# Expert weights in twelve 1 MB transfers instead of six of 2 MB, in a Mixture-of-Experts decoder layer

## The chip, the core and the metric

One core of one Trainium2 chip runs the whole program. The metric is the device time of one execution in microseconds (us), from launch to the last output. The kernel before takes 1163.84 us, the median of 3 runs (1163.27 to 1166.18).

## The reference

One layer of a hybrid decoder trunk for 256 prompt tokens and 8 x 8 sample tokens, 320 in all, of width 1024. First a mixer (a projection `u = x @ w_in`, a gated short convolution, a gated linear recurrence, `@ w_out`, a LayerNorm). Then a Mixture of Experts: each token goes to 4 of 32 experts, and this part takes most of the time. All data are float32.

```python
g = xblk @ wg[e] + bg[e]
up = xblk @ wu[e] + bu[e]
g = jnp.minimum(g, SWIGLU_LIMIT)
up = jnp.clip(up, -SWIGLU_LIMIT, SWIGLU_LIMIT)
glu = g * jax.nn.sigmoid(SWIGLU_ALPHA * g)
return ((up + 1.0) * glu) @ wd[e] + bd[e]
```

Each expert has three matrices (gate, up, down) of 1024 x 1024 float32, 4 MB each, so 12 MB an expert and 384 MB for the 32. Every expert is read once from device memory.

## The kernel before

The mixer runs from 0 to about 184 us. While it runs, the six slots of `ring` serve the projection weights first and then take the matrices of expert 0.

The experts run after it as a loop of *units*. A unit is one expert and up to 64 of its tokens. There are 33 units for 32 experts: one expert has more than 64 tokens and takes two units, one after the other, on the same weights. A unit on TensorE is: gate product, first half; the result sum of the unit before (`combine`); gate product, second half; up product, two halves; gathering of the next unit's tokens (L1146); some transposes; down product, two halves (L1193 is the matmul of all six halves).

`ring` holds one expert: 6 slots of 16 KB a partition, 2 MB each. Slots 0 and 1 are the two halves of the gate matrix, 2 and 3 of up, 4 and 5 of down. In a slot a partition holds 4 whole rows of the matrix, which lie one after the other in device memory, so that a slot is 128 runs of 16 KB. There is no second buffer: a slot is loaded with the next expert's half as soon as the last unit of the present expert has finished its matmuls on it.

The sync engine (SP) issues all weight loads from one queue, in slot order. For each slot it waits until TensorE has counted that slot as used (`half_used` for a first half, `gate_done`, `up_done`, `y_done` for a second), then issues the load (L268, L269). TensorE in turn waits at the head of each half for the load's arrival (L1187), in `product`. `PRIOR` only corrects the count for the loads that the same slots took during the mixer.

GpSimd loads two small bias rows per unit (L369) on its own queue. Everything else of a unit lies on VectorE, ScalarE and GpSimd beside TensorE.

Of the kernel before, what the change touches and what calls it, by code (L numbers as in the profile page):

```python
# [27 lines left out]
SLOTW = 4 * D  # L28
NSLOT = 6
# [17 lines left out]
LOGIT_BANKS = [1, 7, 3]  # L47
SUM_BANKS = [(5, 6), (7, 4), (2, 2)]
SUM_ORDER = (0, 1, 2)
PRIOR = [0, 0, 0, 3, 2, 2]  # L50


def hybrid_layer(nc, a):
# [3 lines left out]
    with ExitStack() as ctx:  # L57
# [3 lines left out]
        def sem(name):  # L61
            return ctx.enter_context(nc.semaphore(name))


        ring = sb("ring", [P, NSLOT, SLOTW])
# [94 lines left out]
        xTu = carve(P, HALF)  # L160
        hTu = carve(P, HALF)
# [30 lines left out]
            "ln2_centred ln2_var ln2_rstd ln2_norm out_dma dve_step act_step pool_step").split()}  # L192
        slot_loaded = [sem(f"slot_loaded{i}") for i in range(NSLOT)]
        x_in, x1_ok, ln2_ok = ([sem(f"{n}{t}") for t in range(3)] for n in ("x_in", "x1_ok", "ln2_ok"))
        half_used = [sem(f"half_used{m}") for m in range(3)]
        product_done = ["gate_done", "up_done", "y_done"]

        block = ctx.enter_context(nc.Block())
        w_in_v = a["w_in"][0].rearrange("(c p) n -> p c n", p=P)
# [4 lines left out]
        def slot_src(s, e):  # L204

            m = experts[s // 2]
            rows = m[e, (s % 2) * HALF:(s % 2 + 1) * HALF, :] if isinstance(e, int) else \
                m[bass.ds(e, 1), (s % 2) * HALF:(s % 2 + 1) * HALF, :].rearrange("o k n -> (o k) n")
            return rows.rearrange("(p c) n -> p (c n)", p=P)

        def slot(s):
            return ring[:, s, :].rearrange("p (c n) -> p c n", n=D)
# [8 lines left out]
        @block.sync  # L221
        def _(sp):

            for t, (t0, n) in enumerate(TILES):
                src = a["x_prompt"][0, t0:t0 + n, :] if t < 2 else a["x_sample"].rearrange("b s d -> (b s) d")
                sp.dma_start(x[0:n, t, :], src).then_inc(x_in[t], 16)

            for i, (g, s) in enumerate(IN_GROUPS[:3]):
                first_col = g * CW
                if i == 0:  # L230
                    first_col += 2 * P
                    sp.dma_start(ring[:, s, :].rearrange("p (c n) -> p c n", n=CW)[:, :, 0:2 * P],
                                 w_in_v[:, :, g * CW:first_col]).then_inc(S["first_cols"], 16)
                if i == 1:
                    sp.wait_ge(S["params_in"], 16 * 11)
                sp.dma_start(ring[:, s, :].rearrange("p (c n) -> p c n", n=CW)[:, :, first_col - g * CW:CW],
                             w_in_v[:, :, first_col:(g + 1) * CW]).then_inc(slot_loaded[s], 16)

            for s in range(3):
                sp.dma_start(ring[:, s, :], slot_src(s, 0)).then_inc(slot_loaded[s], 16)  # L240
            for i, (g, s) in enumerate(IN_GROUPS[3:]):
                sp.wait_ge(S["proj_done"], CT * (i + 1))
                sp.dma_start(ring[:, s, :].rearrange("p (c n) -> p c n", n=CW),
                             w_in_v[:, :, g * CW:(g + 1) * CW]).then_inc(slot_loaded[s], 16)
            sp.wait_ge(S["proj_done"], 3 * CT)
            sp.dma_start(slot(5), w_out_v[:, CT:CH, :]).then_inc(slot_loaded[5], 16)
            sp.wait_ge(S["proj_done"], 4 * CT)
            sp.dma_start(slot(3), w_out_v[:, 0:CT, :]).then_inc(slot_loaded[3], 16)
            for s, done, count in ((4, "proj_done", 5 * CT), (5, "lru_psum", 3), (3, "out_psum", 3)):
                sp.wait_ge(S[done], count)  # L250
                sp.dma_start(ring[:, s, :], slot_src(s, 0)).then_inc(slot_loaded[s], 16)
            for t in range(3):
                sp.wait_ge(x1_ok[t], 1)

            sp.wait_ge(S["out_psum"], 3)
            sp.dma_start(down_bias, a["exp_b_down"][0].rearrange("e (a n) -> e a n", a=4))\
                .then_inc(S["down_bias_in"], 16)
            for v, name in ((ln_g, "ln2_g"), (ln_b, "ln2_b")):
                sp.dma_start(v[:, :], a[name].partition_broadcast(P).rearrange("p o n -> p (o n)"))\
                    .then_inc(S["ln2_in"], 16)  # L260
            sp.wait_ge(S["tab_ok"], 1)

            def expert_load(e, before):

                used = sp.value_load(units_through[0:1, before], min_val=1, max_val=MAXU)
                for s in range(NSLOT):

                    sp.wait_ge(half_used[s // 2] if s % 2 == 0 else S[product_done[s // 2]], used)  # L268
                    sp.dma_start(ring[:, s, :], slot_src(s, e)).then_inc(slot_loaded[s], 16)  # L269

            expert_load(1, slice(0, 1))
            with sp.Fori(2, NE) as e:
                expert_load(e, bass.ds(e - 1, 1))
            for t in (1, 0, 2):
                t0, n = TILES[t]
                sp.wait_ge(ln2_ok[t], 1)
                dst = a["y_prompt"][0, t0:t0 + n, :] if t < 2 else a["y_sample"].rearrange("b s d -> (b s) d")
                sp.dma_start(dst, total[0:n, t, :]).then_inc(S["out_dma"], 16)
            sp.wait_ge(S["out_dma"], 48)
            sp.wait_ge(S["states_dma"], 96)  # L280
# [707 lines left out]
        def _(pe):  # L988
# [3 lines left out]
            for t, (t0, n) in enumerate(TILES):  # L992
                pe.wait_ge(x_in[t], 16)
                for c in range(CH):
                    b, col = (2 * t + c // 4, (c % 4) * P) if t < 2 else (4, c * n)
                    last = nc.tensor.transpose(bank[b][:, col:col + n], x[0:n, t, c * P:(c + 1) * P],
                                               ident[0:n, 0:n])
# [32 lines left out]
            for gi, (g, s) in enumerate(IN_GROUPS):  # L1030
                seen[s] += 1
                w = ring[:, s, :].rearrange("p (c n) -> p c n", n=CW)
                for j in range(CT):
# [7 lines left out]
                    for c in range(CH):  # L1041
                        last = mm(bank[j][:, 0:T], w[:, c, j * P:(j + 1) * P], xT[:, c, :],  # L1042
                                  start=c == 0, stop=c == CH - 1)
# [33 lines left out]
            for t in range(3):  # L1077
# [3 lines left out]
                if t == 0:  # L1081
# [3 lines left out]
                    for j in range(CT):  # L1085
                        last = nc.tensor.transpose(bank[6][0:OUTS, j * P:(j + 1) * P], states[:, j, 0:OUTS],
                                                   ident[:, :])
# [48 lines left out]
            for t, (t0, n) in enumerate(TILES):  # L1136
                last = mm(bank[6][:, 3 * NE:4 * NE], ones_bf[0:n, :], chosen[0:n, t, :],
                          start=t == 0, stop=t == 2)
# [38 lines left out]
            for t, (t0, n) in enumerate(TILES):  # L1177
                last = nc.tensor.transpose(bank[5][0:NE, t0:t0 + n], gate_of[0:n, t, :], ident[0:n, 0:n])
# [2 lines left out]
            pe.wait_ge(S["tab_ok"], 1)  # L1181
            n_last = pe.value_load(last_unit[0:1, 0:1], min_val=NE - 1, max_val=MAXU - 1)

            def product(b, m, left, s, e, between=None):

                for hf in range(2):
                    pe.wait_ge(slot_loaded[2 * m + hf], e * 16 + 16 * (PRIOR[2 * m + hf] + 1))  # L1187
                    w = slot(2 * m + hf)
                    for c in range(4):
                        lhsT = left[:, c * P + hf * UT:c * P + hf * UT + UT]  # L1190
                        end = hf == 1 and c == 3
                        for side in range(2):
                            last = mm(bank[b][side * UT:(side + 1) * UT, :], lhsT,  # L1193
                                      w[:, c, side * HALF:(side + 1) * HALF],
                                      start=m == 2 and hf == 0 and c == 0, stop=end, skip_group_check=True)
                    if hf == 0:
                        last.then_inc(half_used[m], 1)
                        if between:
                            between()
                last.then_inc(S[s], 1)  # L1200

            def biased(b, m):

# [30 lines left out]
            def unit(u, e, results):  # L1234

                pe.wait_ge(S["xu_ok"], u + 1)
                pe.wait_ge(S["gu_split"], u + 1)
                pe.wait_ge(S["gate_free"], u + 1)
                biased(0, 0)
                product(0, 0, xTu, "gate_done", e, between=results)  # L1240
                biased(1, 1).then_inc(S["gu_bias_used"], 1)
                product(1, 1, xTu, "up_done", e)
                pe.wait_ge(S["parts_ok"], 3)
                pe.wait_ge(S["low_zero"], 1)
                pe.wait_ge(S["member_ok"], u + 2)
                gather()
                pe.wait_ge(S["total_ok"], u * 3 + 3)
                pe.wait_ge(S["gated_ok"], u + 1)
                for t, (t0, n) in enumerate(TILES):
                    last = nc.tensor.transpose(bank[5][:, t0:t0 + n], gated[0:n, t, :], ident[0:n, 0:n])  # L1250
                last.then_inc(S["spread_psum"], 1)
                pe.wait_ge(S["hid_ok"], u + 1)
                transposed(4, hid, "hu_psum")
                pe.wait_ge(S["rows_ok"], u + 2)
                transposed(3, x_rows, "xu_psum")
                pe.wait_ge(S["hu_ok"], u + 1)
                product(2, 2, hTu, "y_done", e)

            pe.wait_ge(S["sel_ok"], 3)
            unit(0, 0, gated_biases)  # L1260
# [31 lines left out]
```

## Time and profile before

| what | us |
|---|---|
| median of 3 runs | 1163.84 |
| the profiled execution | 1164.26 |
| its span, first to last instruction | 1162.6 |
| TensorE matmuls, busy | 1086.0 (93%) |
| weight transfers, all loads of the sync queue | 86.5% of 16 engines' span |
| VectorE busy | 513.0 (44%) |
| GpSimd busy | 338.2 (29%) |
| ScalarE busy | 198.5 (17%) |

The page divides the span into 40 slices of 29 us and gives for each how busy every engine was and how many GB/s the 16 transfer engines moved. Its chain of waits follows the work back from the last instruction; there a "DMA" piece runs from the issue of a transfer to its landing. A matmul busy on the page is not a matmul at its peak: its end is modelled, and float32 matmuls appear as two records each, so a half product of 8 matmuls is 16 records.

### The profile page before, as it was taken

How to read it: one execution, taken by the hardware profiler on the slowest of the kernel's cores; microseconds unless marked ns; L12 is line 12 of the kernel's file. 1: busy time of each engine (PE TensorE's matmuls, PEld its weight loads, DVE VectorE, ACT ScalarE, POOL GpSimd, SP SyncE). 2: the span in 40 equal slices, each digit the busy share in tenths (PEclk: the TensorE clock that was granted, in tenths of full speed). 3: DMA queues.
4: the chain of work that ended last, by engine and by line, in shares of the span. 5: the costliest groups of instructions: out<-in, count | busy, mean ns of one | idle time of the engine just before them, and what ended most of it. 6: DMA issues, size and time to landing. Idle time of an engine off the chain costs nothing.

```text
span 1162.6 us, 14222 instructions
## 1 busy us (share of the span) xinstructions
PE 1086.0 (93%) x5219; PEld 436.7 (38%) x5220; DVE 513.0 (44%) x763; ACT 198.5 (17%) x322; POOL 338.2 (29%) x260
## 2 busy tenths in 40 slices
PE   7999947999999999999999999999999999999993
PEld 5766422333333333333333333333333333333330
DVE  4236386444444444444444444444444444444445
ACT  1151041111111111111111111011111111111111
POOL 2001131333333333333333333333333333333331
PEclk9999967999999999999999999999999999999997
DMA  9923233999999859999999999999999999999971
GB/s 319 358 73 145 77 114 102 429 426 429 428 428 427 366 219 427 428 430 426 429 427 429 427 429 427 429 428 428 428 428 429 427 429 427 429 428 429 427 334 45
DMA packets 41130, 423.29 MB, mean 364 GB/s; under 512 B 7839, under 2 KB 10015, under 8 KB 16542
## 3 DMA queue, kind: packets, MB, share of 16 engines
q1 hardware_dynamic: 36112, 421.15, 86.5%
q10 hardware_dynamic: 2766, 1.69, 0.5%
q0 software_dynamic: 2240, 0.30, 0.2%
q8 instruction: 7, 0.11, 0.0%
q14 instruction: 5, 0.04, 0.0%
HBM read 421.69 MB, written 1.42 MB: 364 GB/s over the span
## 4 chain that ended last, share of the span: by engine, by line
PE 61%; DMA 32%; DVE 4%; issue 1%; ACT 1%; SPq 0%
PE bank L1193 39%; DMA ring<-in_exp_w_up 31%; PE bank L1042 8%; PE bank L1229 5%; PE bank L1062 3%; PE bank L1146 3%; PE bank L1163 1%; ACT area L593 1%; PE bank L1250 1%; DMA ring<-in_w_in 1%; PE bank L1205 1%; PE bank L1155 0%; DVE area L960 0%; PE bank L1217 0%; PE bank L1023 0%
## 5 line engine op out<-in xcount | busy, mean ns | idle before, releaser
L1193 PE MATMUL bank<-ring,area 128*64 128x512 f32 x3168 | 713.9, 598 | 17.0 <-ACT area L593 8.9
L1193 PEld LDWEIGHTS bank<-ring,area 128*64 128x64 f32 x3168 | 225.0, 137 | 457.8 <-issue 427.6
L943 DVE TENSOR_TENSOR area<-bank,area 128x512 f32<-128x512 f32 (+1 forms) x204 | 128.4, 684 | 400.4 <-PE bank L1229 393.0
L382 POOL TENSOR_TENSOR bias_parts<-area,zero_col 2x1024 bf16<-2x1024 f32 x34 | 64.1, 1887 | 618.4 <-PE bank L1205 612.4
L886 DVE TENSOR_SCALAR member<-iota_s,unit_base,area 128x64 bf16<-128x64 f32 x99 | 130.1, 1367 | 0.0
L1229 PE MATMUL bank<-area 64*128 64x512 f32 (+1 forms) x396 | 98.8, 615 | 0.8 <-ACT area L599 0.8
L1042 PE MATMUL bank<-xT,ring 128*128 128x320 f32 x320 | 90.1, 442 | 2.6 <-DMA ring<-in_w_in 2.6
L393 POOL TENSOR_TENSOR bias_parts<-area,bias_parts 2x1024 bf16<-2x1024 f32 x34 | 78.8, 2317 | 4.9
L385 POOL TENSOR_TENSOR area<-area,bias_parts 2x1024 f32<-2x1024 f32 x34 | 72.6, 2136 | 5.2 <-POOL bias_parts L382 0.5
L589 ACT ACTIVATE area<-area 128x512 f32<-128x512 f32 x33 | 20.8, 631 | 311.4 <-DVE area L951 311.4
L1042 PEld LDWEIGHTS bank<-xT,ring 128*128 128x128 f32 x320 | 62.1, 195 | 28.9 <-issue 4.5
L390 POOL TENSOR_TENSOR bias_parts<-area,zero_col 2x1024 bf16<-2x1024 f32 x34 | 64.1, 1886 | 2.1
L591 ACT COPY area<-bank 128x512 f32<-128x512 f32 x33 | 19.4, 587 | 256.0 <-PE bank L1146 256.0
L1146 PE MATMUL bank<-area,member 128*64 128x512 bf16 x528 | 62.6, 379 | 0.0
L599 ACT COPY area<-bank 128x512 f32<-128x512 f32 x33 | 19.3, 586 | 214.2 <-PE bank L1193 214.2
L957 DVE TENSOR_SCALAR area<-bank 128x512 f32<-128x512 f32 x33 | 22.8, 691 | 74.2 <-PE bank L1193 74.2
L1229 PEld LDWEIGHTS bank<-area 64*128 64x128 f32 (+1 forms) x396 | 29.2, 167 | 68.1 <-issue 68.1
L1163 PE MATMUL bank<-ident,area 128*128 128x128 f32 x268 | 41.7, 298 | 10.3 <-DVE area L960 9.9
L892 DVE TENSOR_SCALAR area<-member,area 128x128 f32<-128x128 bf16 x99 | 42.6, 483 | 19.1 <-PE bank L1250 19.1
L951 DVE TENSOR_SCALAR area<-bank 128x512 f32<-128x512 f32 x33 | 22.8, 692 | 57.0 <-PE bank L1193 57.0
L960 DVE SCALAR_TENSOR_TENSOR area<-area 128x512 f32<-128x512 f32 x33 | 45.9, 1391 | 1.1
L1146 PEld LDWEIGHTS bank<-area,member 128*64 128x64 bf16 x528 | 30.8, 110 | 39.4 <-issue 19.7
(225 smaller groups left out, 549.8 us busy)
## 6 DMA issues: line engine op xcount, KB each, us to landing
ring<-in_exp_w_gate SPq DMA_DIRECT2D x64, 2048.0 KB, 21.2
ring<-in_exp_w_up SPq DMA_DIRECT2D x64, 2048.0 KB, 22.6
ring<-in_exp_w_down SPq DMA_DIRECT2D x64, 2048.0 KB, 20.7
ring<-in_w_in SPq DMA_DIRECT2D x4, 2048.0 KB, 15.8
ring<-in_w_out SPq DMA_DIRECT2D x2, 2048.0 KB, 7.8
ring<-in_w_in SPq DMA_DIRECT2D x2, 1024.0 KB, 11.2
x<-in_x_prompt SPq DMA_DIRECT2D x2, 512.0 KB, 4.0
out_y_prompt<-area SPq DMA_DIRECT2D x2, 512.0 KB, 3.1
```

The source lines that it names most:

```text
L382: g.tensor_tensor(bias_parts[0:2, :, :], whole, zero, ALU.add).then_inc(S["high_ok"], 1)
L385: g.tensor_tensor(rest, whole, bias_parts[0:2, :, :], ALU.subtract).then_inc(S["rest_ok"], 1)
L390: g.tensor_tensor(bias_parts[32:34, :, :], rest, zero_32, ALU.add).then_inc(S["mid_ok"], 1)
L393: g.tensor_tensor(bias_parts[64:66, :, :], rest, bias_parts[32:34, :, :], ALU.subtract)\
L886: last = v.tensor_scalar(dst[:, t, :], iota_s[:, :], unit_base[:, u], place[:, t, e], ALU.add, ALU.is_equal)
L943: last = v.tensor_tensor(total[0:n, t, cols], src, total[0:n, t, cols], ALU.add)
L960: v.scalar_tensor_tensor(hid, up_clip, 1.0, g_min, ALU.add, ALU.mult).then_inc(S["hid_ok"], 1)
L1042: last = mm(bank[j][:, 0:T], w[:, c, j * P:(j + 1) * P], xT[:, c, :], start=c == 0, stop=c == CH - 1)
L1146: last = mm(bank[3][side * UT:(side + 1) * UT, :], member[:, k // 3, :], x_parts[:, k, side * HALF:(side + 1) * HALF], start=k == 0, stop= ...
L1163: last = nc.tensor.transpose(bank[b][:, c * P:(c + 1) * P], src.rearrange("p (k c) -> p c k", c=4)[:, c, :], ident[:, :])
L1193: last = mm(bank[b][side * UT:(side + 1) * UT, :], lhsT, w[:, c, side * HALF:(side + 1) * HALF], start=m == 2 and hf == 0 and c == 0, stop ...
L1229: last = mm(b[0:n, :] if t < 2 else b[UT * h_:UT * h_ + UT, :], spread[UT * h_:UT * h_ + UT, t0:t0 + n], y_rows[UT * h_:UT * h_ + UT, :], ...
```

## The change

Each 2 MB slot is now loaded by two transfers of 1 MB, called quarters (a quarter of a matrix). Quarter 0 of a slot is the first 8 KB of each partition (rows 0 and 1 of its four), quarter 1 the last 8 KB. In device memory the 128 runs of a quarter are 8 KB long, 16 KB apart. Each quarter has its own semaphore of arrival (`quarter_loaded`) and its own semaphore of release (`quarter_used`; the last quarter of a matrix keeps the old name). TensorE waits before matmuls c = 0 and c = 2 of each half, and counts after c = 1 and c = 3. The matmuls, their order and the layout in `ring` are the same. With own semaphores for the arrival of experts' quarters, `PRIOR` is gone. The loads of expert 0 during the mixer are halved too.

```diff
-PRIOR = [0, 0, 0, 3, 2, 2]
...
-        half_used = [sem(f"half_used{m}") for m in range(3)]
-        product_done = ["gate_done", "up_done", "y_done"]
+        quarter_loaded = [[sem(f"quarter_loaded{s}_{i}") for i in range(2)] for s in range(NSLOT)]
+        quarter_used = [[sem(f"quarter_used{m}_{q}") for q in range(3)] + [S[n]]
+                        for m, n in enumerate(("gate_done", "up_done", "y_done"))]
...
+        def quarter(s, i):
+            return ring[:, s, i * SLOTW // 2:(i + 1) * SLOTW // 2]
+
+        def quarter_src(s, i, e):
+            return slot_src(s, e)[:, i * SLOTW // 2:(i + 1) * SLOTW // 2]
...
             for s in range(3):
-                sp.dma_start(ring[:, s, :], slot_src(s, 0)).then_inc(slot_loaded[s], 16)
+                for i in range(2):
+                    sp.dma_start(quarter(s, i), quarter_src(s, i, 0)).then_inc(quarter_loaded[s][i], 16)
...
                 used = sp.value_load(units_through[0:1, before], min_val=1, max_val=MAXU)
                 for s in range(NSLOT):
-
-                    sp.wait_ge(half_used[s // 2] if s % 2 == 0 else S[product_done[s // 2]], used)
-                    sp.dma_start(ring[:, s, :], slot_src(s, e)).then_inc(slot_loaded[s], 16)
+                    for i in range(2):
+                        sp.wait_ge(quarter_used[s // 2][s % 2 * 2 + i], used)
+                        sp.dma_start(quarter(s, i), quarter_src(s, i, e)).then_inc(quarter_loaded[s][i], 16)
...
-            def product(b, m, left, s, e, between=None):
+            def product(b, m, left, e, between=None):
 
                 for hf in range(2):
-                    pe.wait_ge(slot_loaded[2 * m + hf], e * 16 + 16 * (PRIOR[2 * m + hf] + 1))
                     w = slot(2 * m + hf)
                     for c in range(4):
+                        if c % 2 == 0:
+                            pe.wait_ge(quarter_loaded[2 * m + hf][c // 2], e * 16 + 16)
                         lhsT = left[:, c * P + hf * UT:c * P + hf * UT + UT]
                         end = hf == 1 and c == 3
                         for side in range(2):
                             last = mm(bank[b][side * UT:(side + 1) * UT, :], lhsT,
                                       w[:, c, side * HALF:(side + 1) * HALF],
                                       start=m == 2 and hf == 0 and c == 0, stop=end, skip_group_check=True)
-                    if hf == 0:
-                        last.then_inc(half_used[m], 1)
-                        if between:
-                            between()
-                last.then_inc(S[s], 1)
+                        if c % 2 == 1:
+                            last.then_inc(quarter_used[m][hf * 2 + c // 2], 1)
+                    if hf == 0 and between:
+                        between()
```

On the sync engine, inside the loop over experts 2 to 31, the loads of one expert stood so before (each waits for the release named behind it; 4096 is the floats of a partition):

```order
L269 ISA [waits half_used0]
L269 DMA ring<-in_exp_w_gate 128x4096
L269 ISA [waits gate_done]
L269 DMA ring<-in_exp_w_gate 128x4096
L269 DMA ring<-in_exp_w_up 128x4096 [waits half_used1]
L269 DMA ring<-in_exp_w_up 128x4096 [waits up_done]
L269 DMA ring<-in_exp_w_down 128x4096 [waits half_used2]
L269 DMA ring<-in_exp_w_down 128x4096 [waits y_done]
```

Now, for the last gate quarter, up and down:

```order
L277 ISA [waits quarter_used0_2]
L277 DMA ring<-in_exp_w_gate 128x2048
L277 ISA [waits gate_done]
L277 DMA ring<-in_exp_w_gate 128x2048
L277 DMA ring<-in_exp_w_up 128x2048 [waits quarter_used1_0]
L277 DMA ring<-in_exp_w_up 128x2048 [waits quarter_used1_1]
L277 DMA ring<-in_exp_w_up 128x2048 [waits quarter_used1_2]
L277 DMA ring<-in_exp_w_up 128x2048 [waits up_done]
L277 DMA ring<-in_exp_w_down 128x2048 [waits quarter_used2_0]
L277 DMA ring<-in_exp_w_down 128x2048 [waits quarter_used2_1]
L277 DMA ring<-in_exp_w_down 128x2048 [waits quarter_used2_2]
L277 DMA ring<-in_exp_w_down 128x2048 [waits y_done]
```

The order of the matrices in the queue is as it was; each load became two of half the width, each with a wait of its own for its own release.

On TensorE, in the loop over units, from the first half of up to the gathering, the rows before were (a wait stands with the first matmul behind it):

```order
L1193 MATMUL bank<-ring,area 64x512 [waits slot_loaded2]
L1193 MATMUL bank<-ring,area 64x512 x7
L1187 REGISTER_ALU
L1193 MATMUL bank<-ring,area 64x512 [waits slot_loaded3]
L1193 MATMUL bank<-ring,area 64x512 x7
L1245 REGISTER_ALU [waits low_zero,parts_ok]
L1146 MATMUL bank<-area,member 64x512 [waits member_ok]
```

Now:

```order
L1202 MATMUL bank<-ring,area 64x512 [waits quarter_loaded2_0]
L1202 MATMUL bank<-ring,area 64x512 x3
L1202 MATMUL bank<-ring,area 64x512 [waits quarter_loaded2_1]
L1202 MATMUL bank<-ring,area 64x512 x3
L1202 MATMUL bank<-ring,area 64x512 [waits quarter_loaded3_0]
L1202 MATMUL bank<-ring,area 64x512 x3
L1202 MATMUL bank<-ring,area 64x512 [waits quarter_loaded3_1]
L1202 MATMUL bank<-ring,area 64x512 x3
L1253 REGISTER_ALU [waits low_zero,parts_ok]
L1154 MATMUL bank<-area,member 64x512 [waits member_ok]
```

The eight matmuls of a half fell into four and four, with a wait for an arrival before each four. Nothing changed its place.

## Rows read from the trace of the kernel before

**Rows 1.** The page: whole span, busiest engines, 40 slices (29 us each) of transfers.

```profile
span 1162.6 us, 14222 instructions
...
PE 1086.0 (93%) x5219; PEld 436.7 (38%) x5220; DVE 513.0 (44%) x763; ACT 198.5 (17%) x322; POOL 338.2 (29%) x260
...
DMA  9923233999999859999999999999999999999971
GB/s 319 358 73 145 77 114 102 429 426 429 428 428 427 366 219 427 428 430 426 429 427 429 427 429 427 429 428 428 428 428 429 427 429 427 429 428 429 427 334 45
```

**Rows 2.** Chain that ended last, near its end: start us, us, what.

```profile
1068.91 25.96 DMA ring<-in_exp_w_up
...
1098.61 25.96 DMA ring<-in_exp_w_up
1124.58 0.04 issue
1124.62 3.68 PE bank L1193 x16
...
1132.70 2.35 PE bank L1193 x9
```

**Rows 3.** The same chain, where its kind changes.

```profile
648.84 6.87 PE bank L1193 x32
...
676.90 6.89 PE bank L1193 x32
683.82 25.02 DMA ring<-in_exp_w_up
```

**Rows 4.** Timeline of the sync engine, 370 to 450 us: start, us, what.

```profile
382.46 3.77 SPq L269 DMA_DIRECT2D ring<-in_exp_w_down  x2
417.76 6.85 SPq L269 DMA_DIRECT2D ring<-in_exp_w_gate  x2
```

**Rows 5.** Stages: length, busy us (count) per engine, clock, DMA share, GB/s.

```profile
400.00:415.00 15.00, 14.73 (x83) 6.11 (x81) 4.48 (x7) 3.00 (x6) 5.90 (x5) 1.00 0.18 77
415.00:430.00 15.00, 15.00 (x71) 4.81 (x68) 8.92 (x11) 1.49 (x2) 4.68 (x4) 1.00 0.70 253
445.00:680.00 235.00, 232.82 (x1162) 85.42 (x1160) 104.45 (x138) 36.55 (x57) 77.53 (x50) 1.00 1.01 428
800.00:1100.00 300.00, 284.20 (x1414) 102.66 (x1410) 125.08 (x162) 44.91 (x70) 94.42 (x64) 1.00 1.01 428
...
1128.00:1132.00 4.00, 3.37 (x27) 1.95 (x24) 3.38 (x5) 0.60 (x2) 2.46 (x2) 1.00 0.10 43
1132.00:1135.00 3.00, 2.73 (x16) 1.14 (x16) 0.00 (x0) 1.39 (x3) 0.00 (x0) 1.00 0.04 16
```

**Rows 6.** Line 269, from 412 us on: its gate loads.

```profile
L269 SPq DMA_DIRECT2D ring<-in_exp_w_gate x48: 332/334/337, 417.8 to 1091.2; - x48
```

**Rows 7.** Transfers of 16 KB runs, 800 to 1100 us: all packets, then by queue.

```profile
DMA packets 9448, 128.39 MB, mean 428 GB/s; under 512 B 1577, under 2 KB 1577, under 8 KB 1617
...
q1 hardware_dynamic: 8807, 128.31, 100.5%
```

**Rows 8.** The same view, 23 to 28 us (w_in, 2 KB runs).

```profile
DMA packets 960, 1.93 MB, mean 387 GB/s; under 512 B 16, under 2 KB 16, under 8 KB 960
```

**Rows 9.** The same view, 73 to 77 us and 91 to 95 us (w_out, 4 KB runs).

```profile
DMA packets 409, 1.68 MB, mean 420 GB/s; under 512 B 0, under 2 KB 0, under 8 KB 408
...
DMA packets 403, 1.65 MB, mean 413 GB/s; under 512 B 0, under 2 KB 0, under 8 KB 403
```

**Rows 10.** Timeline of TensorE, 430 to 450 us: start, us, what.

```profile
434.90 7.09 PE L1193 MATMUL bank<-ring,area 128*64 128x512 f32 x32 [0.27 <-ACT area L593]
...
442.04 3.61 PE L1193 MATMUL bank<-ring,area 128*64 128x512 f32 x16
```

**Rows 11.** Issues, KB each, us to landing: w_out (page), one expert half, 128 to 140 us.

```profile
ring<-in_w_out SPq DMA_DIRECT2D x2, 2048.0 KB, 7.8
...
ring<-in_exp_w_down SPq DMA_DIRECT2D x1, 2048.0 KB, 7.8
```

More of the change, by code:

```diff
@@ L250, in _ @@
                 sp.wait_ge(S[done], count)
-                sp.dma_start(ring[:, s, :], slot_src(s, 0)).then_inc(slot_loaded[s], 16)
+                for i in range(2):
+                    sp.dma_start(quarter(s, i), quarter_src(s, i, 0)).then_inc(quarter_loaded[s][i], 16)
             for t in range(3):
@@ L266, in expert_load @@
                 for s in range(NSLOT):
-                    sp.wait_ge(half_used[s // 2] if s % 2 == 0 else S[product_done[s // 2]], used)
-                    sp.dma_start(ring[:, s, :], slot_src(s, e)).then_inc(slot_loaded[s], 16)
+                    for i in range(2):
+                        sp.wait_ge(quarter_used[s // 2][s % 2 * 2 + i], used)
+                        sp.dma_start(quarter(s, i), quarter_src(s, i, e)).then_inc(quarter_loaded[s][i], 16)
             expert_load(1, slice(0, 1))
@@ L1239, in unit @@
                 biased(0, 0)
-                product(0, 0, xTu, "gate_done", e, between=results)
+                product(0, 0, xTu, e, between=results)
                 biased(1, 1).then_inc(S["gu_bias_used"], 1)
-                product(1, 1, xTu, "up_done", e)
+                product(1, 1, xTu, e)
                 pe.wait_ge(S["parts_ok"], 3)
@@ L1256, in unit @@
                 pe.wait_ge(S["hu_ok"], u + 1)
-                product(2, 2, hTu, "y_done", e)
+                product(2, 2, hTu, e)
             pe.wait_ge(S["sel_ok"], 3)
```

## The prediction

> **What bounds the kernel now.** I read the page first. TensorE shows 93% busy, but from slice 8 on the transfers run at 426 to 430 GB/s, except in slices 14 and 15 (366 and 219) [rows 1]. Both could be the bound, so I went to the chain of waits. It has two kinds of stretch. Up to 683 us it is TensorE alone: one unit every 28.06 us (648.84 to 676.90) [rows 3]. From 683.82 us on it runs through the transfers: a load of the second half of up takes 25.96 us from issue to landing, TensorE then takes 3.68 us for its 16 records and so frees the slot, and the next load of the same slot is issued. One turn takes 29.70 us (1068.91 to 1098.61) [rows 2]. The 25.96 us are mostly queueing, since two such loads alone on the engines land in 7.8 us [rows 11].
>
> The rate decides. An expert is 6 x 2.097 = 12.58 MB; at 428 GB/s [rows 5] it takes 29.4 us, and the turn takes 29.70. The rest, 0.3 us, is with a few engines that run behind: when the last loads run out, the share is 0.10 and then 0.04 between 1128 and 1135 us, some 1.6 and 0.6 of 16 engines [rows 5]. A load has landed only when its slowest engine is done.
>
> So TensorE uses up an expert 1.64 us faster than it is loaded. The ring's lead hides that for some units; then TensorE waits. The lead was last filled where one expert takes two units: no slot is freed in the first of them, the transfers fall to 0.18 busy [rows 5], and the sync queue issues nothing between the last down load, before 387 us, and 417.76 us [rows 4]. From there to the end it is one unbroken stream: 48 gate loads [rows 6], so 24 experts, at 428 GB/s in both long stretches [rows 5]. The end of the kernel is therefore: start of the stream (417.76 us, set by TensorE), plus 24 experts at the transfer rate, plus what TensorE still has to do behind the last up load.
>
> **The change, part by part.** The sum has three terms.
>
> *Earlier start.* The first 8 records of a half free its first quarter. From 32 records in 7.09 us and 16 in 3.61 [rows 10], 16 more take 3.48 us and 8 take 1.74. The stream's first load is thus issued 1.74 us before 417.76; all first quarters behind it are released as much earlier, so the stream stays that much ahead. Gain 1.74 us.
>
> *Later need.* The last wait for a weight is that for the last half of up: landed 1124.58 us, TensorE starts at 1124.62 and needs 3.68 us [rows 2]. Now the last quarter lands then, and the quarter before it landed a quarter of a half turn earlier: one transfer of 2 MB costs 29.70 / 6 = 4.95 us of stream, one of 1 MB 2.5 us, more than the 1.74 us of its matmuls. Only 8 records are left behind the last arrival. Gain 1.74 us. What is late next is down: two more halves land 2 x 4.95 = 9.9 us behind up, at 1134.5 us in the old times. The down product starts at 1132.70 [rows 2], would start at 1131.0, and needs its last quarter 3 x 1.74 = 5.2 us later, at 1136.2: 1.7 us in hand. The gain stands.
>
> *More packets.* A load of 128 runs is 128 packets, 8 on each of the 16 engines, and a 4-byte packet on each engine for the semaphore: between 800 and 1100 us the sync queue's 8807 packets are 7831 of 16 KB (128.31 MB) and 976 small ones, one to eight [rows 7]. With 8 KB runs the same bytes need 16 packets and two small ones. An engine gets 6 x 8 + 6 = 54 packets more per expert, 24 x 54 = 1296 in the stream. What does a packet cost beside its bytes? No row shows 8 KB runs, so I bound it by full stretches of other sizes. At 428 GB/s a 16 KB packet takes an engine 16 x 16384 / 428 = 612.5 ns [rows 7]. At 2 KB, 944 packets in 5 us are 16 x 5000 / 944 = 84.7 ns each [rows 8]; eight of them take 678 ns, and the 65 ns more for 7 more packets are 9.3 ns each. At 4 KB, 413 and 420 GB/s are 158.7 and 156.0 ns [rows 9]; four take 635 or 624, so 7.4 or 3.8 ns each; these are windows of 4 us in a single load, where a few packets at the edges matter. The size does not seem to change the price per packet, as it would with a fixed step in each. I take 8.4 ns, the middle of 9.3 and 7.4, also for a semaphore's packet. Loss 1296 x 8.4 ns = 10.9 us.
>
> [...]
>
> *Edits with no price.* Six more waits per unit on TensorE: in the 32 records of down there is already a wait with its load landed, and these take 7.09 us, no more than twice 3.61 [rows 10]. If each cost the 0.04 us between a landing and its matmuls [rows 2], the 9 units before the stream would be 9 x 6 x 0.04 = 2.2 us longer; I take nothing, and keep 2.2 for the range. Behind 417 us TensorE waits anyhow. Six more issues per expert on the sync queue are 6 x 0.33 us [rows 6] in a turn of 29.70, in which it mostly waits; behind it stand only the next loads. The halved loads of expert 0 in the mixer land long before 184 us, when they are first needed. TensorE's clock is at full grant in both long stretches (1.00) [rows 5]; a little more waiting per unit could let it fall at times, but a slower product in the stream hides behind 25 us of queued loads.
>
> Sum: 10.9 - 1.74 - 1.74 = +7.4 us. The profiled execution would go from 1164.26 us (span 1162.6) to 1171.7. It stood 0.4 above the median of 3 runs, so I forecast 1163.84 + 7.4 = 1171.2 us. Seen by stages: an expert grows by 54 x 8.4 ns = 0.45 us, the turn from 29.70 to 30.15.
>
> Does the stream still begin at TensorE's pace? Before, a lead of (683.82 - 417.76) / 28.06 = 9.5 units x 1.64 = 15.6 us was used up before the first wait. Between the start of the experts and the two-unit expert there are only 8 units, which now cost 8 x 2.09 = 16.7 us, against a lead of 15.6 + 3.5 = 19.1. It holds by 2 us.
>
> **Rivals.** A difference under 0.3%, 3.5 us, can't be told from none here.
>
> *A cheap packet.* The 420 GB/s row gives 3.8 ns [rows 9]. At that price 1296 packets lose 4.9 us, 3.5 are gained, and the time is 1163.84 + 1.4 = 1165.2: no change that can be told. Against it stand 387 GB/s at 2 KB [rows 8], the steadier stretch, which 3.8 ns would put at 411 (76.1 + 3.8 = 79.9 ns a packet). I give it 0.14. [...]
>
> *Packets cost nothing.* Then only the two gains are left: 1163.84 - 3.5 = 1160.4, faster by 0.30%, just at the border. For it: alone on the engines, a 2 MB load in 4 KB runs lands in 7.8 us, as one in 16 KB runs does (7.8) [rows 11], with four times the packets. Against: a lone load leaves engines with time between packets (0.70 and less where the queue isn't full [rows 5]), the stream doesn't. I give it 0.10, most of it faster.
>
> *The gains don't come, or TensorE pays.* The quarters save nothing if the two halves of a slot land together, because the slow engines work them one right behind the other and the last one sets both, or if the six waits cost 2.2 us in front of the stream. At 9.3 ns that is 12.1 us lost and nothing gained: 1175.9. It decides from the point where the wait for the second quarter of up is as long as that for the first. Against it: the slow engines work in order too, and a quarter is 2.5 us of work for them. I give it 0.10.
>
> *The change doesn't do what it says.* If 8 KB runs were cut or joined in the same packets as before, nothing would be lost. The packets of 16 KB, 4 KB and 2 KB runs each have the size of their run [rows 7 to 9], so I count that in the rival above.
>
> **How the numbers follow.** Forecast 0.66, own range 1167 to 1173.5 (7.4 and 9.3 ns with the gains give 1169.9 and 1172.4, with a microsecond or so for the scatter of runs and some more below towards 3.8 ns). With the two rivals below it and the one above it at the probabilities given, the range that leaves out 2 in 10 at most is 1162.5 to 1175: it leaves out the free packet nearly whole and the far end of the last rival. Faster by over 0.3%: 0.07, most of the free packet. Within 0.3%: 0.03 from it, 0.12 from the cheap packet and 0.02 from the forecast's low end, 0.17. Slower: 0.76.
>
> **What would show it.** In the profile after: in the long stretches 8 KB packets at about 422 GB/s instead of 428 (8192 x 16 / 310.5 ns); turns of 30.15 us; the first load behind the two-unit expert issued near 416.0 us; behind the last landing of up 8 records, some 1.9 us, instead of 3.68; units of 28.06 us before that, and the first wait for a landing again near 680 us. If the rate stays at 428, the packet's price was wrong, and the time falls to the border of 1160. If units before 417 us are longer than 28.06, the waits cost TensorE something. If the last two landings of up come together, the last rival holds.

## The result and the profile after

| | median, us | range | runs |
|---|---|---|---|
| kernel before | 1165.32 | 1163.27 to 1166.18 | 5 |
| kernel changed | 1171.26 | 1170.08 to 1172.69 | 5 |

The ratio is 1.0055 with a 95% interval of 1.0043 to 1.0068, so the changed kernel is slower by 6.4 us (5.0 to 7.9); the two medians alone differ by 5.9. The forecast was +7.4 us, and 1171.2 us in all. The profiled execution of the changed kernel took 1172.69 us, its span 1171.1.

The page of the changed kernel, against [rows 1]:

```profile
span 1171.1 us, 14622 instructions
...
DMA  9913233999999969999999999999999999999981
GB/s 309 363 73 144 76 113 119 412 421 421 421 421 421 376 257 421 421 421 421 421 423 421 421 421 421 422 421 421 421 421 422 422 421 421 421 421 421 421 372 48
```

The transfers run at 421 GB/s where they ran at 428, in the same slices. Stages (length, busy us and count per engine, clock, DMA share, GB/s), against [rows 5]:

```profile
445.00:680.00 235.00, 233.44 (x1166) 84.46 (x1164) 103.42 (x137) 37.04 (x58) 76.60 (x49) 1.00 1.01 421
800.00:1100.00 300.00, 283.96 (x1386) 98.16 (x1384) 119.33 (x159) 44.89 (x70) 89.39 (x60) 1.00 1.01 421
```

In the two long stretches the transfer engines are as busy as before (1.01) and still move less (421 GB/s for 428). What the sync queue's transfers were made of between 800 and 1100 us, against [rows 7]:

```profile
DMA packets 17984, 126.42 MB, mean 421 GB/s; under 512 B 2523, under 2 KB 2523, under 8 KB 2563
...
q1 hardware_dynamic: 17344, 126.34, 101.2%
```

Twice the packets (17344 for 8807) carry 1.5% less. The chain near its end, against [rows 2] (start us, us, what):

```profile
1105.63 2.10 SPq L277
...
1107.82 27.17 DMA ring<-in_exp_w_up
1134.99 0.04 issue
1135.04 1.96 PE bank L1202 x8
1137.02 0.70 DVE area L965
1137.75 1.89 DVE area L968
```

and the piece of the chain before that answers to L965:

```profile
1128.32 0.70 DVE area L957
```

From the last landing of up (1134.99) to the start of VectorE's next operation (1137.02) are 2.03 us; before, 3.74 (1124.58 to 1128.32). The turn has to be read over several experts, since this chain goes partly through other loads. An earlier piece of it is

```profile
895.97 28.13 DMA ring<-in_exp_w_up
```

It lands at 924.10, seven turns ahead of 1134.99, so a turn is 30.13 us; before, 29.70. Where the chain changes its kind, against [rows 3]:

```profile
621.85 6.87 PE bank L1202 x32
...
649.84 6.89 PE bank L1202 x32
656.75 26.26 DMA ring<-in_exp_w_up
```

A unit takes 27.99 us (621.85 to 649.84; before 28.06), so the six more waits cost TensorE nothing. The first wait for a landing on the chain comes at 656.75 us, one unit earlier than the 683.82 of before, since the lead is used up faster. The sync engine near the two-unit expert, against [rows 4]:

```profile
382.47 5.48 SPq L277 DMA_DIRECT2D ring<-in_exp_w_down  x4
417.69 8.55 SPq L277 DMA_DIRECT2D ring<-in_exp_w_gate  x4
```

These rows divide the difference of the two spans, 8.5 us:

| stage | before | after | difference |
|---|---|---|---|
| start to the first expert product | 184.79 | 186.76 | +2.0 |
| to the first load behind the two-unit expert | 232.97 | 230.93 | -2.0 |
| stream: that load to the last landing of up | 706.81 | 717.30 | +10.5 |
| last landing of up to the end | 38.0 | 36.1 | -1.9 |

(The first product's start is the chain's row of it, 184.79 and 186.76 us; both loads and landings stand above and in [rows 2, 4].) The first stage is most likely not the change. The mixer of this execution had a lower granted clock of TensorE, 0.88 of full on the mean of 120 to 128 us, during `w_out`'s products; the execution of before had 1.00 there:

```profile
120.00:128.00 8.00, 8.00 (x22) 2.97 (x22) 1.41 (x2) 0.00 (x0) 0.00 (x0) 0.88 0.01 2
```

A later run with the same mixer code (releases by quarter, below) had 1.00 there and its first expert product at 183.44 us, and the kernel before itself, in 15 runs, spreads from 1163.26 to 1169.18 us with mean clocks of 0.970 to 0.978. Without the first stage the sum is +6.6, and the ratio gives +6.4.

### The profile page after: what moved, and what is told of

Same layout as the page of the kernel before. It is cut to its first block, busy times and chain, and to the rows that moved or that the text cites. A ratio compares the mean times of both kernels' runs of the same rounds, so it can differ in the third digit from the quotient of the medians.

```text
span 1171.1 us, 14622 instructions
## 1 busy us (share of the span) xinstructions
PE 1092.2 (93%) x5219; PEld 429.5 (37%) x5220; DVE 508.3 (43%) x763; ACT 198.4 (17%) x322; POOL 337.3 (29%) x260
## 4 chain that ended last, share of the span: by engine, by line
PE 59%; DMA 29%; SPq 5%; DVE 5%; issue 1%; ACT 1%
PE bank L1202 36%; DMA ring<-in_exp_w_up 19%; DMA ring<-in_exp_w_gate 9%; PE bank L1050 8%; PE bank L1237 5%; SPq L277 5%; PE bank L1070 3%; PE bank L1154 3%; PE bank L1171 1%; ACT area L601 1%; PE bank L1258 1%; DMA ring<-in_w_in 1%; PE bank L1213 1%; DVE area L968 1%; PE bank L1163 0%
## 5 line engine op out<-in xcount | busy, mean ns | idle before, releaser
L1202 PEld LDWEIGHTS bank<-ring,area 128*64 128x64 f32 x3168 | 218.0, 137 | 474.7 <-issue 387.2
L393 POOL TENSOR_TENSOR area<-area,bias_parts 2x1024 f32<-2x1024 f32 x34 | 72.6, 2134 | 5.3 <-POOL bias_parts L390 0.5
L965 DVE TENSOR_SCALAR area<-bank 128x512 f32<-128x512 f32 x33 | 22.8, 692 | 84.0 <-PE bank L1202 84.0
L900 DVE TENSOR_SCALAR area<-member,area 128x128 f32<-128x128 bf16 x99 | 39.1, 448 | 15.3 <-PE bank L1258 15.3
L968 DVE SCALAR_TENSOR_TENSOR area<-area 128x512 f32<-128x512 f32 x33 | 44.7, 1354 | 1.1
```

The lines of the kernel that those rows point to most:

```text
L393: g.tensor_tensor(rest, whole, bias_parts[0:2, :, :], ALU.subtract).then_inc(S["rest_ok"], 1)
L968: v.scalar_tensor_tensor(hid, up_clip, 1.0, g_min, ALU.add, ALU.mult).then_inc(S["hid_ok"], 1)
L1202: last = mm(bank[b][side * UT:(side + 1) * UT, :], lhsT, w[:, c, side * HALF:(side + 1) * HALF], start=m == 2 and hf == 0 and c == 0, stop ...
```

## The experiments

All medians below stand beside runs of the kernel before on the same chip: 1164.22 us for the first four (11 runs), 1164.79 for the last three (15 runs). "Stream" is always the time from the first load behind the two-unit expert to the last landing of up, 706.8 us before and 717.3 changed. The stages of a run are read from its one profiled execution.

**Packets or transfers.** The changed kernel has both more packets and more transfers. Theory 1 puts a price on each packet, theory 2 on each transfer. Two kernels keep six transfers of 2 MB and change only the length of their runs, by giving a partition other rows of the matrix.

```diff
-            return rows.rearrange("(p c) n -> p (c n)", p=P)
+            return rows.rearrange("(a p b) n -> p a (b n)", a=2, b=2)    # 8 KB runs
+            return rows.rearrange("(c p) n -> p c n", p=P)                # 4 KB runs, the second kernel
```

> Six transfers of 2 MB per expert with whole-half arrivals and releases, as before, but each in 8 KB runs: a partition of a slot holds two pairs of neighbouring rows, 256 rows apart, and the transposes of the tokens follow that order, so that the result is the same. Theory 1 (the price is per packet, 8.2 ns, worked out from the 10.5 us by which the stream grew over 1278 packets): 48 more packets per expert, none more for semaphores, 1152 in 24 experts, +9.4 us on the kernel before, so about 1174.7 us, 422 GB/s, turns of 29.70 + 0.39 = 30.09 us. Theory 2 (the price is per transfer, 73 ns, and the run length is free): the number of transfers is that of before, 1165.3 us, 428 GB/s. For the queue: if the sync engine's issues block (over 1 us each) as they do in the changed kernel, the limit is one of packets queued; if they stay at 0.33 us, it is one of transfers.

Measured: 1174.7 us, ratio 1.0088 (1.0071 to 1.0105), +10.2 us. Its chain, packets and first load behind the two-unit expert:

```profile
1078.06 26.39 DMA ring<-in_exp_w_up
...
1108.19 26.41 DMA ring<-in_exp_w_up
```

```profile
DMA packets 17026, 126.46 MB, mean 422 GB/s; under 512 B 1560, under 2 KB 1560, under 8 KB 1600
...
q1 hardware_dynamic: 16386, 126.37, 101.1%
```

```profile
417.23 6.88 SPq L269 DMA_DIRECT2D ring<-in_exp_w_gate  x2
```

Turn 30.13 us (1078.06 to 1108.19), stream 1134.60 - 417.23 = 717.4 us: with six transfers the stream has grown as much as with twelve. The run length alone costs it 10.6 us. Theory 2 is out. The sync engine's issues did not block (0.37 to 0.40 us each) with some 5 transfers of 16 packets per engine queued.

> As the run with six transfers in 8 KB runs, but in 4 KB runs (a partition of a slot holds four rows 128 apart; the transposes follow). Theory 1: 144 more packets per engine and expert than before, 3456 in 24 experts at 8.2 ns, +28.3 us on the kernel before: about 1193.6 us, a turn of 30.9 us, 412 GB/s; the lead runs out near the two-unit expert, which may add a microsecond. If the price were 3.8 ns a packet: +13 us. Theory 2: 1165.3 us.

Measured: 1198.95 us, ratio 1.0296 (1.0272 to 1.0319), +34.5 us; 28.3 and perhaps one more were expected. Packets, first load behind the two-unit expert, and two stretches of the chain:

```profile
DMA packets 31479, 122.80 MB, mean 409 GB/s; under 512 B 1482, under 2 KB 1482, under 8 KB 31479
```

```profile
420.31 6.88 SPq L269 DMA_DIRECT2D ring<-in_exp_w_gate  x2
```

```profile
377.67 24.35 DMA ring<-in_exp_w_up
```

```profile
1129.24 5.11 SPq L269
1134.45 24.35 DMA ring<-in_exp_w_up
```

The stream took 1158.80 - 420.31 = 738.5 us, 31.7 more than before. Most of the rest is that the lead ran out early: this chain goes through a landing already at 377.67 us, ahead of the two-unit expert, and the stream began 236.5 us after the first product (183.86) instead of 233.0, 3.5 us later. Together these are 35.2 us; the two spans differ by 33.5, as the mixer and the tail were 0.9 and 0.7 us shorter here.

The price of a packet follows three times. Up to the last landing of up a stream holds 23 2/3 experts. 48 more data packets per engine in each are 1136, for 10.5 us (changed kernel) and 10.6 us (six transfers): 9.2 and 9.3 ns a packet. 144 more are 3408, for 31.7 us: 9.3 ns. The full rates say nearly the same: a packet takes an engine 612.5 ns at 16 KB (428 GB/s), 311 at 8 KB (421.5, from 126.46 MB in 300 us) and 160.2 at 4 KB (409), so 9.5 and 9.4 ns more for each packet added. The order of the addresses is not what costs: the changed kernel reads 8 KB runs that lie 16 KB apart, the one with six transfers reads them one behind the other, and their streams take 717.3 and 717.4 us.

**What the finer grain gives.** This is the changed kernel with waits and releases of whole halves:

```diff
-                        if c % 2 == 0:
-                            pe.wait_ge(quarter_loaded[2 * m + hf][c // 2], e * 16 + 16)
+                        if c == 0:
+                            pe.wait_ge(quarter_loaded[2 * m + hf][0], e * 16 + 16)
+                            pe.wait_ge(quarter_loaded[2 * m + hf][1], e * 16 + 16)
...
-                        sp.wait_ge(quarter_used[s // 2][s % 2 * 2 + i], used)
+                        sp.wait_ge(quarter_used[s // 2][s % 2 * 2 + 1], used)
```

> The changed kernel with its twelve transfers in 8 KB runs, but TensorE waits for both quarters of a half before its first matmul, and the sync engine waits for the release of a whole half before it issues either quarter. It takes away both gains of the finer grain and leaves the price. Forecast's theory: 3.5 us more than the changed kernel, 1171.3 + 3.5 = 1174.8 us; the first load behind the two-unit expert is issued 1.74 us later against the start of its unit, and 3.7 instead of 2.0 us lie between the last landing of up and VectorE. Rival (the finer grain gains nothing): 1171.3 us as the changed kernel.

Measured: 1175.87 us, ratio 1.0095 (1.0074 to 1.0116), its median 4.6 us over that of the changed kernel. First load behind the two-unit expert, and the end of the chain:

```profile
419.05 7.35 SPq L277 DMA_DIRECT2D ring<-in_exp_w_gate  x4
```

```profile
1110.46 25.93 DMA ring<-in_exp_w_up
...
1136.53 3.67 PE bank L1203 x16
...
1140.22 0.70 DVE area L965
```

The first expert product began at 186.38 us, so the stream began 232.7 us later (changed kernel: 230.9), and from landing (1136.39) to VectorE (1140.22) lie 3.8 us (2.0). That is 1.7 + 1.8 = 3.5 us, as forecast; the medians' 4.6 has an uncertainty of over 2 us. The stream itself took 717.3 us, against 717.4 with six transfers of runs of the same length: six more semaphore packets per engine and expert and twice the transfers cost nothing that can be seen.

**Each half of it alone.** First only the change to the release, then only that to the wait.

```diff
-                        sp.wait_ge(quarter_used[s // 2][s % 2 * 2 + i], used)
+                        sp.wait_ge(quarter_used[s // 2][s % 2 * 2 + 1], used)
```

> The changed kernel (twelve transfers, 8 KB runs) with arrivals by quarter, but releases by half: the sync engine waits for the release of a whole half before it issues either quarter. Forecast's theory: the later need is kept (2.0 us from the last landing of up to VectorE), the earlier start is lost: first load behind the two-unit expert about 232.7 us after the start of the experts' first product, as in the kernel before, instead of 230.9. Time 1.74 us over the changed kernel and 1.8 us under the run that halved both: by the ratios so far, 1164.2 x 1.0055 + 1.7 = 1172.3 us. Rival (arrival and release gain only together, because the ring hands slots round in a circle): 1174 to 1175 us as with both halved.

Measured: 1172.57 us, ratio 1.0067 (1.0053 to 1.0081). The same rows:

```profile
421.26 7.35 SPq L277 DMA_DIRECT2D ring<-in_exp_w_gate  x4
```

```profile
1111.28 27.23 DMA ring<-in_exp_w_up
...
1138.55 1.96 PE bank L1202 x8
...
1140.54 0.70 DVE area L965
```

```diff
-                        if c % 2 == 0:
-                            pe.wait_ge(quarter_loaded[2 * m + hf][c // 2], e * 16 + 16)
+                        if c == 0:
+                            pe.wait_ge(quarter_loaded[2 * m + hf][0], e * 16 + 16)
+                            pe.wait_ge(quarter_loaded[2 * m + hf][1], e * 16 + 16)
```

> The other half of it: releases by quarter, TensorE waits for both quarters of a half. Forecast's theory: 230.9 us from the first product to the first load behind the two-unit expert, but 3.8 us from the last landing of up to VectorE; 1172.3 us as well. Rival as in the run with arrivals by quarter: 1174 to 1175 us.

Measured: 1174.01 us, ratio 1.0084 (1.0069 to 1.0099). The same rows:

```profile
414.25 8.55 SPq L277 DMA_DIRECT2D ring<-in_exp_w_gate  x4
```

```profile
1104.92 26.31 DMA ring<-in_exp_w_up
...
1131.37 3.67 PE bank L1203 x16
...
1135.06 0.70 DVE area L965
```

The experts' first products began at 188.73 and 183.44 us. So arrivals by quarter: 232.5 us to the stream, 2.0 us behind the landing (1138.51 to 1140.54). Releases by quarter: 230.8 and 3.8 (1131.23 to 1135.06). Each does its own part and not the other's. The times alone (+7.8 and +9.8 us over the kernel before, beside +6.4 with both gains and +11.1 with none) lie between those two, but they don't settle it: +8.1 was expected of each, and each has 1.6 us or more of uncertainty; with the profiled spans, 1174.6 and 1169.1, they would lie the wrong way round, since the two executions' mixers differed by 5.3 us.

**Twelve transfers in 16 KB runs.** Each takes 64 of the 128 partitions; its source is cut the same way, and waits and releases are by whole halves.

```diff
-            return ring[:, s, i * SLOTW // 2:(i + 1) * SLOTW // 2]
+            return ring[i * UT:(i + 1) * UT, s, :]
```

> Twelve transfers of 1 MB, but in 16 KB runs: each takes 64 of the 128 partitions of a slot; whole-half waits and releases. Only the semaphores' packets are more than before, 6 per engine and expert. Theory 1 (per packet): 144 x 8.2 ns = +1.2 us, 1166.5 us, 428 GB/s less 0.2%. Theory 2 (per transfer): +10.5 us as the stream of the changed kernel, 1175.8 us. If the engines share 64 partitions worse than 128, both are off and the time is much longer; the number of packets per transfer tells that.

Measured: 2084.75 us, ratio 1.7895. Neither theory is tested by it, since the rate fell for another reason:

```profile
DMA packets 5155, 63.50 MB, mean 212 GB/s; under 512 B 1262, under 2 KB 1262, under 8 KB 1282
...
q1 hardware_dynamic: 4835, 63.46, 100.7%
```

The transfers ran at 212 GB/s, half of 428, with the queue's share of the engines at 100.7% (100.5% before). Between 800 and 1100 us a 16 KB packet took 1.24 us on the mean (3873 of them) where it took 0.615 in the kernel before (7831). Why it did, no run shows.

**A version that beats both.** Halves in 16 KB runs as before; only the last expert's second halves of up and of down come in quarters. TensorE's last unit stands behind its loop and waits for each of these quarters by itself.

```diff
+                    if e is LAST and s in early:          # s is 3 or 5
+                        for i, arrived in ((0, early[s]), (1, slot_loaded[s])):
+                            part = slice(i * SLOTW // 2, (i + 1) * SLOTW // 2)
+                            sp.dma_start(ring[:, s, part], slot_src(s, e)[:, part]).then_inc(arrived, 16)
...
-            with pe.Fori(0, n_last) as before:
+            with pe.Fori(0, n_last - 1) as before:
                 ...
+            unit(n_last, NE - 1, lambda: combine(n_last - 1, SUM_ORDER), last_unit_=True)
```

> A version meant to beat both: the kernel before (six transfers of 2 MB, 16 KB runs, halves) for all experts, and only for the last expert the second halves of up and of down come as two transfers of 1 MB each with an arrival of their own; TensorE's last unit stands apart from the loop for it. It takes the gain of the later need once and pays 8 to 18 packets instead of 1296. Forecast's theory: 1.74 - 0.1 = 1.6 us under the kernel before, so 1162.6 us where that one is at 1164.2; 2.0 us from the last landing of up to VectorE instead of 3.7; 428 GB/s. If the second wait in the loop or the unrolled last unit costs something, no change, 1164.2.

Measured: 1162.18 us, ratio 0.9977 (0.9968 to 0.9987): 2.7 us faster than before (1.5 to 3.7). The last unit in the timeline (start, us, what):

```profile
1119.67 7.04 PE L1207 MATMUL bank<-ring,area 128*64 128x512 f32 x32
...
1125.97 1.88 POOL L400 TENSOR_TENSOR bias_parts<-area,zero_col 2x1024 bf16<-2x1024 f32 x1
...
1127.48 0.93 DVE L970 SCALAR_TENSOR_TENSOR area<-area 128x512 f32<-128x512 f32 x1
1128.00 2.40 POOL L403 TENSOR_TENSOR bias_parts<-area,bias_parts 2x1024 bf16<-2x1024 f32 x1
...
1130.36 7.09 PE L1207 MATMUL bank<-ring,area 128*64 128x512 f32 x32 [0.20 <-ACT area L603]
```

and the same stretch of VectorE and GpSimd in the kernel before:

```profile
1128.48 2.12 POOL L393 TENSOR_TENSOR bias_parts<-area,bias_parts 2x1024 bf16<-2x1024 f32 x1
1129.05 2.10 DVE L960 SCALAR_TENSOR_TENSOR area<-area 128x512 f32<-128x512 f32 x1
```

TensorE there, in the kernel before:

```profile
1120.16 3.60 PE L1193 MATMUL bank<-ring,area 128*64 128x512 f32 x16
1124.62 3.65 PE L1193 MATMUL bank<-ring,area 128*64 128x512 f32 x16 [0.86 <-DMA ring<-in_exp_w_up]
```

Up now runs its 32 records without a wait, 7.04 us from its start to its end (1119.67 to 1126.71) where it took 8.14 (1120.16 to 1128.30). That is worth 1.1 us, the 0.86 that TensorE had waited and some 0.2 of the interruption, not the 1.74 expected: the forecast of this run forgot that a wait can't be shortened below nothing. The other part is one step further. VectorE's product of L960 (L970 here) takes 0.93 us where it took 2.10. In the kernel before it began 0.57 us behind the start of GpSimd's operation of L393 and ended 0.55 us behind its end (1130.60 to 1131.15). Here it comes ahead of that operation (L403) and has only the last 0.37 us of the one before it (L400) in its way; it ends 0.56 us behind that one's end (1127.85 to 1128.41). So the down product starts 3.65 us behind the end of up (1126.71 to 1130.36, on the chain's rows) instead of 4.40 (1128.30 to 1132.70). From the stream's first load to the down product are 714.9 us before (417.76 to 1132.70) and 713.0 here (417.38 to 1130.36): 2.0 of the 2.7 us are seen, the rest is within the interval. No run has the last unit behind the loop without the quarters; that the quarters do it is read from the wait that is gone.

## Why the prediction was right

- **The bound.** Right: one stream of 24 experts, full before and after. Its turn went from 29.70 to 30.13 us (30.15 forecast), with the rate at 421 GB/s (422 forecast). The first wait came at 656.75 us, earlier than the 680 named as a sign.
- **The number.** The forecast of 1171.2 us stood on 1163.84 for the kernel before, which measured 1165.32 with two more runs, so that 1171.26 comes so near to it is luck. The difference, 7.4 us for 6.4, is the fair measure.
- **More packets.** The count was right: a load of 2 MB in 16 KB runs is 128 packets and 16 of 4 bytes, in 16 rows of nine, and the 4-byte ones go with the rises of its semaphore (first point of the last section). The sync queue of the changed kernel has 49152 packets of 8 KB in its whole trace for 24576 of 16 KB, and 6416 of 4 bytes for 3344, 16 more for each of its 192 further transfers. The loss was right in sum, 10.5 us for 10.9, by two errors that cancel, which is luck too. A data packet costs 9.3 ns, not 8.4: the longer row, 2 KB runs at 387 GB/s [rows 8], had it, and mixing in the 4 us windows of single loads [rows 9] only blurred it (the 420 GB/s row gives 3.9 ns, not 3.8; nothing hangs on that). A semaphore's packet costs nothing to be seen, where the sum had 1.2 us for them: six transfers and twelve have streams of 717.4 and 717.3 us. 1152 x 9.3 ns is 10.7 us for the whole stream.
- **Earlier start.** Right: 1.74 us forecast. Between kernels that differ in the release alone it is 1.6 (232.5 to 230.9, with arrivals by quarter) and 1.9 us (232.7 to 230.8, with arrivals by half).
- **Later need.** Right in size, 1.71 us (3.74 to 2.03), but the prediction left a condition unasked: such a gain can't exceed the wait that TensorE has there. The last two quarters of up landed 2.49 us apart (1132.50 and 1134.99), and TensorE waited for each:

```profile
1132.55 1.94 PE L1202 MATMUL bank<-ring,area 128*64 128x512 f32 x8 [0.31 <-DMA ring<-in_exp_w_up]
1135.04 1.94 PE L1202 MATMUL bank<-ring,area 128*64 128x512 f32 x8 [0.55 <-DMA ring<-in_exp_w_up]
```

  With halves the wait ahead of up's second half was shorter than 1.74 us, 0.86 before and 1.12 with both halved. What made room for the whole gain is that the quarters stand in every turn. TensorE is done with up 1.8 us sooner in each, and so comes to the next up 1.8 us sooner: its first half began 6.36 us ahead of up's last landing in the changed kernel (1128.63 to 1134.99), and 4.58 with both halved (1131.81 to 1136.39). With arrivals by quarter alone it is 6.38, with releases by quarter alone 4.56.

```profile
1128.63 3.60 PE L1202 MATMUL bank<-ring,area 128*64 128x512 f32 x16
```

```profile
1131.81 3.60 PE L1203 MATMUL bank<-ring,area 128*64 128x512 f32 x16
1136.53 3.65 PE L1203 MATMUL bank<-ring,area 128*64 128x512 f32 x16 [1.12 <-DMA ring<-in_exp_w_up]
```

  The last version has quarters in its last expert alone, so it could gain no more there than the wait of before.
- **Edits with no price.** Right for TensorE (27.99 us a unit). Its clock stayed at 1.00 in both long stretches. In the run with 64 partitions a transfer, where it was busy for 185.7 of the 300 us from 800 on (284.0 in the changed kernel), it was 0.80. For the sync engine the time was right and the reason wrong, see the last section.
- **The rivals.** The cheap packet (3.8 ns, 1165.2 us) fell by the two kernels with other runs; it leaned on the 420 GB/s of a 4 us window [rows 9]. The free packet fell with it. The last rival, that the gains don't come, fell by the stages of the three kernels that took the gains away singly and together.
- **The whole.** +7.4 forecast, +6.4 by the ratio, +6.6 by the stages. The tail gave 1.9 and the start 2.0 where 1.74 each were forecast. In the tail VectorE's product (L968, L960 before) took 1.89 us for 2.11, since it began 0.80 us behind the start of GpSimd's operation instead of 0.57 (last section). At the start most units were 0.07 us shorter, 0.5 in sum, while the first half of gate took 0.2 longer (5.16 for 4.93); why a unit is shorter stays open.

## What to carry to other kernels

Where a stream of transfers is what ends last, price a finer cut by its packets first. Count the packets that it adds for one engine over the whole stream. For the price of one, take two stretches of the same trace in which the queue is full and the runs have different lengths, and see how much longer the same bytes take in the shorter runs. The gain of a finer cut comes once per stream, at its start and at its end (1.7 and 1.8 us here), not once per transfer. So cut only the transfers at the ends and leave the long middle in the longest runs; but look first how long the consumer really waits there, for a cut at the very end alone gives back no more than that wait and what follows from it.

## What the runs showed of the hardware

- What a load is made of, from one that is alone on the engines (kernel before, first half of down, issued at 108.43 us; packets from 108 to 120 us):

```profile
DMA packets 144, 2.10 MB, mean 175 GB/s; under 512 B 16, under 2 KB 16, under 8 KB 16
```

  The trace gives each packet its size, start and length: 128 have 16384 bytes and 16 have 4. Put end to end, each begun within 6 ns of where one before it ended, they make 16 rows, as many as there are engines, and every row is eight packets of 16 KB and then one of 4 bytes. The load's semaphore rose 16 times, between 115.25 and 116.21 us, each time 0.31 to 0.37 us behind the end of a 4-byte packet, taken in order. The last rise is the landing.
- A load lands with its slowest engine. For the last half of up before, 14 of the 16 rises came between 1117.00 and 1117.96 us, the other two at 1121.14 and 1124.58, and TensorE began at 1124.62. The slow ones work in order too: in the changed kernel the last rises of up's four quarters came at 1127.55, 1130.03, 1132.50 and 1134.99 us, 2.5 us apart.
- The price per packet is the same between 16, 8 and 4 KB: 9.3 ns an engine, whether the packets belong to one transfer or to two. The small packets for the semaphores add nothing to be seen (126.37 MB in 300 us with six transfers, 126.34 to 126.39 with twelve).
- Transfers into 64 neighbouring partitions ran at 212 GB/s with the engines shown busy (100.7%), those into 128 at 428.
- An issue on the sync engine can block. In the changed kernel half of up's loads behind 680 us took 2.1 us or more (1105.63 above), the longest 4.4; all gate loads of the stream had taken 0.33 or 0.34 before [rows 6]. At 1105.63 some 11 transfers of 8 packets per engine were queued (27.17 us to the landing, 2.5 a transfer). With 4 KB runs the medians behind 680 us are 4.4 to 4.9 us (1129.24 above), the longest 8.6, with some 5 transfers of 32 packets queued. With some 5 transfers of 16 packets none blocked. So neither a number of transfers nor one of packets explains all three, and the limit stays open. It cost the stream nothing, as the engines' share stayed at 1.01 and the stream is as long as with six transfers, though the chain shows 5% of the span on the sync engine.
- VectorE's 128 x 512 product of L960, with both inputs in `area`, waits for a GpSimd operation that is running when it starts. Each trace but that of the 64 partitions has 33 of it, 264 in all. In 257 such an operation was running, and the product ended 0.54 to 0.56 us behind that operation's end, whether it took 0.93 us in all or 2.65. In the other seven, where none was running or one ended within some 0.1 us of the start, it took 0.69. Ending a wait can so be worth more than the wait, when it moves a step out of such a neighbour's way.
